# Sampled tokens out of the last product's matmuls in three of eight weight units: their rows gathered by indirect DMA and added by VectorE, which also makes the low half of those weights

## The chip, the cores and the metric

The kernel runs on one core of a Trainium2 chip. The metric is device time in microseconds (us). The kernel before took 2319.9 us, the median of 3 runs (2318.9 to 2320.13).

## The reference, cut to what matters

One layer for 256 prompt tokens and 32 sampled tokens (8 sequences of 4), 288 columns in all. It has an attention and pooling part, a norm, and then an expert layer, which takes most of the time:

```
s = einsum('chpe,hpne->chpn', q, sub_keys)     # 8 heads, 2 halves, 128 keys
ts, ti = top_k(s, 16)                          # ... then the best 16 of 256 pairs
idx  = i1 * 128 + i2                           # 8 heads x 16 experts a token, of 16384
gate = softmax(cs)
a    = einsum('cd,chkd->chk', xc, peer_u[idx])
act  = gelu(a) * gate
out  = einsum('chk,chkd->cd', act, peer_v[idx])
```

Each token uses 128 of the 16384 rows of `peer_u` and `peer_v` (2048 numbers a row, fp32). All is fp32, and the kernel keeps close to that precision.

## The kernel before, in words

**Dense instead of gathered.** The kernel does not gather. It multiplies all 16384 rows of `peer_u` with all tokens, takes gelu, writes that to a scratch tensor in HBM (`gelu_scratch`), multiplies it with a gate matrix that is zero wherever a token did not choose an expert (`gate_scratch`, made on chip from one-hot products), and multiplies the result with all of `peer_v`. The last step is the phase `peer_v`, and the change is there.

**Units.** A weight unit is 128 partitions x 2048 fp32 numbers (1 MB). `peer_v` has 128 units: 16 blocks of 1024 experts, and in each block 8 units, one for each pair of output tiles (a tile is 128 of the 2048 outputs, so there are 16 tiles and 8 pairs). A product of fp32 quality is three fp32r products: weights and activations are each split in a rounded high part and the rest. A unit is two output tiles of 24 matmuls each: 8 k-steps with `w_hi` x `b_hi` (L1412) and `w_hi` x `b_lo` (L1413), then 8 with `w_lo` x `b_hi` (L1418), each 128x128 weights on 288 columns. The result of an output tile is in one of four PSUM banks and is added to `R`.

**Who does what in `peer_v`, for unit u.** SP issues the loads of `raw` in two halves (L629), as soon as the low half of unit u-2 has been made, since `raw`, `w_hi` and `w_lo` have two buffers. ScalarE (ACT) rounds the halves to `w_hi` (L734) once PE has finished unit u-2. GpSimd (POOL) makes `w_lo = raw - w_hi` (L707). VectorE (DVE) adds a finished output tile to `R` (`take`, L1358) and makes the activations of the next block, one of eight tiles a unit (`gate`: multiply L1351, round to `b_hi` L1352, rest to `b_lo` L1353). PE waits for `hi_ready` and `lo_ready` of its unit, and for the bank it writes (`ev_dve`, the addition four output tiles back). SP also loads the next block's gelu and gate pieces (L382). All orders are written out by hand, and each engine runs its own in order.

**Before it.** The routing (top 16, chosen names and gates in `I1`, `I2`, `GA`) is done by DVE during `peer_u`; it signals `r_idx`, PE then transposes the names (L1686), DVE copies them (L1292) and begins the one-hots (L1307 to L1314) for the gate matrix (PE, L1700).

**After it.** The last 8 units run beside the start of the last norm, and after them come its sums (L597, L590, L607) and the output.

Of the kernel before, what the change touches and what calls it, by code (L numbers as in the profile page):

```python
# [118 lines left out]
def const_table():  # L119

    t = np.zeros((P, CONSTS), np.float32)

    def put(name, a):
        t[:, CONST[name][0]:CONST[name][1]] = a

    put("ident", np.eye(P))
    half = HD // 2
    inv = np.float32(10000.0) ** (-np.arange(half, dtype=np.float32) / np.float32(half))
    pos = np.concatenate([np.arange(SEQ), PAST + np.tile(np.arange(DS), DB)]).astype(np.float32)
    ang = (pos[None, :] * inv.astype(np.float32)[:, None]).astype(np.float32)  # L130
# [12 lines left out]
    put("ratio", (w / np.minimum(w, np.arange(16)[None, :] + 1)).astype(np.float32).reshape(1, -1))  # L143
    put("iota", np.arange(128)[None, :])
    return t
# [22 lines left out]
def layer(nc, xT, w_in, w_pool, w_attn, w_out, w_query, keysT, peer_u, peer_v, vecs, consts,  # L168
# [3 lines left out]
    with ctx:  # L172
# [14 lines left out]

        ah, al = (sb(name, [P, KT, T + 4], F32R)[:, :, 0:T] for name in ("a_hi", "a_lo"))
# [20 lines left out]
        F = sb("F", [P, (212863 - 4 * (6 * KT * P + KT * T + 2 * KT * (T + 4) + 2 * KT * TW + VECS + CONSTS + P)) // 4 - 32])  # L209
# [76 lines left out]
        GS, o_ab = carve(o_ab, TOKS, P)  # L286

# [25 lines left out]
        hi_ready, lo_ready = sem("hi_ready"), sem("lo_ready")  # L313
        outs_done = sem("outs_done")
# [54 lines left out]
        def block_piece(sp, b, s, n, i=None):  # L369
# [12 lines left out]
            sp.dma_start(dst, src).then_inc(blk_in[s], 16)  # L382

# [238 lines left out]
        def _(sp):  # L622
# [62 lines left out]
            with sp.Fori(0, BLOCKS // 2 - 1) as i:  # L685
                for s in range(2):
                    for j in range(8):
                        load(peer_v[16 * i + 8 * s + j], UNIT0["peer_v"] + 8 * s, 8 * i, j)
                        if j < 4:
                            block_piece(sp, 2 * i + s + 2, s, j, i)  # L690
            stream(peer_v, UNIT0["peer_v"] + 112, 16, first=112)
# [10 lines left out]
        def _(pool):  # L702
# [266 lines left out]
        def _(ve):  # L969
# [7 lines left out]
            for s in (h_prob, h_ol, g_ev):  # L977
                ve.sem_inc(s, 1)
# [310 lines left out]

            for n, dst in enumerate((I1T, I2T, gT[:, :])):  # L1290
                ve.wait_ge(r_pe, NHALF + n + 1)
                link(ve.tensor_copy(dst, ps[:, 4 + n, 0:T]))  # L1292
# [63 lines left out]
            def take(o, j, i):  # L1356
                ve.wait_ge(outs_done, OUT0["peer_v"] + i + o + 2)
                ve.tensor_tensor(R[:, j, :], R[:, j, :], ps[:, ROT[(o + 2) % 4], 0:T], ALU.add).then_inc(ev_dve, 1)  # L1358
# [7 lines left out]
            def v_block(i, s):  # L1366
# [11 lines left out]
            with ve.Fori(0, BLOCKS // 2 - 1) as i:  # L1378
                own.start(i, 32)
                for s in range(2):  # L1380
                    v_block(i, s)
                own.stop(BLOCKS // 2 - 1)
            v_block(BLOCKS // 2 - 1, 0)
# [13 lines left out]
        def _(pe):  # L1397
            def product(bank, slot, tiles, mh, ml, u, m_wait=None, cols=T):


                out = ps[:, bank, 0:cols]
                for first in range(0, len(tiles), 8):
# [11 lines left out]
                    for n, (t, k) in half:  # L1414
                        if t % 8 == 0:

                            pe.wait_ge(lo_ready, 2 * u + t // 8 + 1)
                        last = pe.matmul(out, wl[:, slot, t * P:t * P + P], mh(k), start=False,  # L1418
                                         stop=(n == len(tiles) - 1))
                last.then_inc(outs_done, 1)  # L1420
# [289 lines left out]

            def v_unit(i, s, j):
                if j == 1:

                    pe.wait_ge(ev_act, ACT_EV0["peer_u"] + 128)
                pairs("peer_v", 16 * i + 8 * s, j,
                      lambda k: bh[:, 8 * s + k, 0:T], lambda k: bl[:, 8 * s + k, 0:T], first=2)
# [7 lines left out]
            with pe.Fori(0, 4) as n:  # L1724
                for j in range(2):
                    pairs("peer_v", 112 + 2 * n, j, a_op(bh), a_op(bl), first=2)
            pe.wait_ge(act_ready, 8 * BLOCKS)
            for j in range(8):
                v_unit(BLOCKS // 2 - 1, 1, j)
# [76 lines left out]
```

## Time and profile before

| | |
|---|---|
| median of 3 runs | 2319.9 us |
| span of the profiled execution | 2318.2 us |
| PE busy | 2301.9 us (99%) |
| DVE, ACT, POOL busy | 1419.4, 882.9, 1702.8 us |
| DMA | 198 GB/s over the span |
| last product (`peer_v`) | from about 1490.4 us to about 2300 us |

The profiled execution is known by its span alone; the median of the runs shown is 1.7 us above it. The span is from the first to the last instruction of the core. "Busy" of PE is pipelined: each matmul record is longer than the distance to the next, so the distance between starts is what counts, and a group of n back-to-back matmuls that is b us long with records of m us has the distance (b - m) / (n - 1).

### The profile page before, as it was taken

To read this page: it belongs to the slowest core of one execution; us is meant where nothing else is said; L and a number is where in the kernel's file an instruction comes from. 1 tells how busy PE (TensorE), PEld (TensorE's weight loads), DVE (VectorE), ACT (ScalarE), POOL (GpSimd) and SP (SyncE) were. 2 spreads that over 40 slices of the span, in tenths; PEclk is the share of its full clock that TensorE was granted. 3 is DMA by queue.
4 is the path that set the end of the run, shared out by engine and by line. 5 is a ranking of instruction groups with operands and counts; after the bars stand their busy time and mean duration, and the time that the engine had idled before them with its cause. 6 is when DMAs were issued, how large, how long until landed. Compare 5 with 4: busy or idle time off the path is not lost.

```text
span 2318.2 us, 48204 instructions
## 1 busy us (share of the span) xinstructions
PE 2301.9 (99%) x17575; PEld 2293.4 (99%) x17575; DVE 1419.4 (61%) x2373; ACT 882.9 (38%) x1109; POOL 1702.8 (73%) x702
## 2 busy tenths in 40 slices
PE   9999999999999999999999999999999999999997
PEld 9999999999999999999999999999999999999997
DVE  3974564355569954656565640766666777666655
ACT  5444453345544443333333333333333333333334
POOL 4876677776677777677676767777777778777775
PEclk9999999999999999999999999999999999999998
DMA  7564446654455555666666668766666666666643
GB/s 255 168 200 146 145 143 206 213 173 154 146 164 194 185 191 184 217 215 211 211 209 213 208 216 257 282 205 206 209 215 220 217 213 206 208 206 217 199 164 114
DMA packets 141275, 458.25 MB, mean 198 GB/s; under 512 B 14448, under 2 KB 37232, under 8 KB 140656
## 3 DMA queue, kind: packets, MB, share of 16 engines
q1 hardware_dynamic: 116944, 416.42, 55.6%
q10 hardware_dynamic: 24264, 40.93, 4.8%
q8 instruction: 44, 0.72, 0.1%
q14 instruction: 23, 0.19, 0.0%
HBM read 416.40 MB, written 43.28 MB: 198 GB/s over the span
## 4 chain that ended last, share of the span: by engine, by line
PE 95%; DVE 4%; ACT 0%; issue 0%; ACTq 0%; DVEq 0%
PE ps L1412 30%; PE ps L1413 30%; PE ps L1418 30%; PE ps L1700 1%; DVE F L1010 1%; PE ps L1453 1%; DVE F L1011 1%; PE ps L1626 1%; PE ps L1645 0%; DVE b_lo L1024 0%; PE ps L1460 0%; DVE R L1039 0%; DVE R L1073 0%; PE ps L615 0%; ACT R L964 0%; PE ps L1551 0%
## 5 line engine op out<-in xcount | busy, mean ns | idle before, releaser
L707 POOL TENSOR_TENSOR w_lo<-raw,w_hi 128x1024 fp32r<-128x1024 f32 x692 | 1694.3, 2470 | 599.4 <-ACT w_hi L734 568.4
L734 ACT ACTIVATE w_hi<-raw 128x1024 fp32r<-128x1024 f32 x690 | 692.8, 1052 | 686.1 <-PE ps L1418 652.5
L1412 PE MATMUL ps<-a_hi,w_hi 128*128 128x288 f32 x3072 | 824.8, 295 | 0.0
L1413 PE MATMUL ps<-a_lo,w_hi 128*128 128x288 f32 x3072 | 822.6, 294 | 0.0
L1412 PE MATMUL ps<-b_hi,w_hi 128*128 128x288 f32 (+1 forms) x2432 | 655.1, 295 | 0.4 <-ACT w_hi L734 0.4
L1413 PE MATMUL ps<-b_lo,w_hi 128*128 128x288 f32 (+1 forms) x2432 | 653.0, 295 | 0.0
L1412 PEld LDWEIGHTS ps<-a_hi,w_hi 128*128 128x128 f32 x3072 | 577.7, 188 | 2.4 <-issue 2.2
L1413 PEld LDWEIGHTS ps<-a_lo,w_hi 128*128 128x128 f32 x3072 | 577.9, 188 | 0.1
L1418 PE MATMUL ps<-a_hi,w_lo 128*128 128x288 f32 x3072 | 467.2, 294 | 0.0
L1412 PEld LDWEIGHTS ps<-b_hi,w_hi 128*128 128x128 f32 x2432 | 457.1, 188 | 0.9 <-issue 0.8
L1413 PEld LDWEIGHTS ps<-b_lo,w_hi 128*128 128x128 f32 x2432 | 457.8, 188 | 0.1
L1418 PEld LDWEIGHTS ps<-a_hi,w_lo 128*128 128x128 f32 x3072 | 424.7, 188 | 0.0
L1418 PE MATMUL ps<-b_hi,w_lo 128*128 128x288 f32 (+1 forms) x2432 | 372.0, 294 | 0.0
L1418 PEld LDWEIGHTS ps<-b_hi,w_lo 128*128 128x128 f32 x2432 | 338.1, 188 | 0.3 <-POOL w_lo L707 0.3
L1358 DVE TENSOR_TENSOR R<-R,ps 128x288 f32<-128x288 f32 x240 | 103.1, 449 | 243.1 <-PE ps L1418 243.1
L906 ACT ACTIVATE F<-ps 128x288 f32<-128x288 f32 x128 | 52.5, 410 | 504.3 <-PE ps L1418 504.2
L1353 DVE TENSOR_TENSOR b_lo<-F,b_hi 128x288 fp32r<-128x288 f32 x128 | 171.3, 1338 | 4.4
L1323 DVE COPY F<-ps 128x512 f32<-128x512 f32 x72 | 49.8, 692 | 199.0 <-PE ps L1700 199.0
L1351 DVE TENSOR_TENSOR F<-F 128x288 f32<-128x288 f32 x128 | 122.7, 959 | 75.5 <-DMA F<-gate_scratch 69.2
L1352 DVE CAST b_hi<-F 128x288 fp32r<-128x288 f32 x128 | 156.6, 1223 | 4.4
L1331 DVE TENSOR_TENSOR g_stage<-ps,F 128x512 f32 (+1 forms) x72 | 81.1, 1127 | 0.1
L801 ACT ACTIVATE F<-ps,vec 128x288 f32 (+1 forms) x32 | 16.0, 501 | 111.7 <-PE ps L1418 111.7
(238 smaller groups left out, 1256.4 us busy)
## 6 DMA issues: line engine op xcount, KB each, us to landing
raw<-in_peer_u SPq DMA_DIRECT2D x256, 512.0 KB, 4.3
raw<-in_peer_v SPq DMA_DIRECT2D x256, 512.0 KB, 4.0
raw<-in_w_in SPq DMA_DIRECT2D x96, 512.0 KB, 3.9
gelu_scratch<-F ACTq DMA_DIRECT2D x32, 576.0 KB, 5.7
gate_scratch<-g_stage ACTq DMA_DIRECT2D x36, 512.0 KB, 6.0
F<-gelu_scratch SPq DMA_DIRECT2D x32, 576.0 KB, 5.7
raw<-in_w_out SPq DMA_DIRECT2D x32, 512.0 KB, 3.7
raw<-in_w_query SPq DMA_DIRECT2D x32, 512.0 KB, 3.7
```

The lines of the kernel that those rows point to most:

```text
L707: pool.tensor_tensor(wl[:, j, s], raw[:, j, s], wh[:, j, s].bitcast(F32), ALU.subtract).then_inc(lo_ready, 1)
L734: act.activation(wh[:, k, s], raw[:, k, s], ACT.Copy).then_inc(hi_ready, 1)
L906: act.activation(ST[:, j // 4, j % 4, :], ps[:, j % 2, 0:T], ACT.Gelu).then_inc(ev_act, 1)
L1323: copied = own.inc(ve.tensor_copy(GS, both[:, :, 1, :]))
L1331: ve.tensor_tensor(to[:, :, :, TOKS * j:TOKS * j + TOKS].rearrange("p a e t -> p t (a e)"), both[:, :, 0, :], GS, ALU.add).then_inc(g_ev, 1)
L1351: link(ve.tensor_tensor(a, a, g, ALU.mult))
L1352: link(ve.tensor_copy(bh[:, 8 * s + e, 0:T], AB[:, s, e, :]))
L1353: ve.tensor_tensor(bl[:, 8 * s + e, 0:T], AB[:, s, e, :], bh[:, 8 * s + e, 0:T].bitcast(F32), ALU.subtract).then_inc(act_ready, 1)
L1358: ve.tensor_tensor(R[:, j, :], R[:, j, :], ps[:, ROT[(o + 2) % 4], 0:T], ALU.add).then_inc(ev_dve, 1)
L1412: pe.matmul(out, w, mh(k), start=(n == 0), stop=False)
L1413: pe.matmul(out, w, ml(k), start=False, stop=False)
L1418: last = pe.matmul(out, wl[:, slot, t * P:t * P + P], mh(k), start=False, stop=(n == len(tiles) - 1))
```

## The change

**Which products shrink.** In each block the last 3 of the 8 units (`dj >= DENSE`, 5) multiply 256 columns, the prompt alone, in place of 288. Their additions to `R` (`take`) have 256 columns too. Block 14 (units 112 to 119) is written as two loops of two units, and there only units 117 and 119 are short (118 is multiplied with 288 columns, and 256 are added). So 14 x 3 + 2 + 3 = 47 units are short, of 128.

**Where the sampled tokens' part comes from.** The 32 tokens x 128 experts are put in 32 slots of 128 partitions. For each slot POOL issues six indirect DMAs, one for each of the 6 output tiles (128 rows of 128 numbers of `peer_v`, 64 KB), and a seventh for the 128 gelu values. Their names are worked out by DVE after the routing. DVE multiplies gelu by gate and adds the slot's rows to `ACC` (128x768). In the last block six small matmuls with a 0/1 matrix (`spread`) sum `ACC` over the partitions of a token into the columns 256 to 288 of the bank. The issues are paced by `outs_done`: 7 for 6.2 output tiles; a slot has one of two buffers (`RING`).

**Who makes `w_lo`.** POOL makes it up to the end of `peer_u` and for the last 8 units of `peer_v`. For the 120 units between DVE does (`lower`), one unit ahead, between `gate` and `take`. SP's loads wait for the new semaphore `lo_dve`; they and the block pieces keep their turn.

The diff, cut to its core:

```diff
+SPARSE = 3
+DENSE = 8 - SPARSE
+ROWS = 2 * SPARSE
+SLOTS = PH * TOPK // 4
+RING = 2
+V_LAST = 120
...
# gpsimd
-            with pool.Fori(FIRST_UNITS // 2, UNITS // 2) as i:
+            with pool.Fori(FIRST_UNITS // 2, UNIT0["peer_v"] // 2) as i:
                 for j in range(2):
                     lower(i, j)
...
+            def paced(k, r):
+                i, m = divmod(k, 5)
+                pool.wait_ge(outs_done, OUT0["peer_v"] + 1 + 32 * i + int(6.2 * (m + r / (ROWS + 1))))
+            for k in range(SLOTS):
+                n = k % RING
+                if k >= RING:
+                    pool.wait_ge(slot_used, k - RING + 2)
+                for r in range(ROWS):
+                    paced(k, r)
+                    pool.indirect_dma_start(VROWS[:, n, r * P:r * P + P], None, v_rows,
+                                            bass.IndirectOffsetOnAxis(ap=VIDX[:, k, r:r + 1], axis=0))\
+                        .then_inc(row_in[n][r], 16)
+                paced(k, ROWS)
+                pool.indirect_dma_start(GELU[:, k:k + 1], None, gelus, ...)\
+                    .then_inc(gelu_in[n], 16)
+            with pool.Fori((UNIT0["peer_v"] + V_LAST) // 2, UNITS // 2) as i:
+                for j in range(2):
+                    lower(i, j)
...
# vector
             def take(o, j, i):
+                n = v_cols(j // 2)
...
+            def lower(u, j):
+                for h in range(2):
+                    ve.wait_ge(hi_ready, 2 * (UNIT0["peer_v"] + u) + h + 1)
+                    s = slice(h * HU, h * HU + HU)
+                    ve.tensor_tensor(wl[:, j, s], raw[:, j, s], wh[:, j, s].bitcast(F32), ALU.subtract)\
+                        .then_inc(lo_dve, 1)
+            def add_slot(i, n):
+                k, b = 10 * i + n, n % RING
+                for r in range(ROWS):
+                    ve.wait_ge(row_in[b][r], 16 * (5 * i + n // RING + 1))
+                ve.wait_ge(gelu_in[b], 16 * (5 * i + n // RING + 1))
+                link(ve.tensor_tensor(GATED[:, b:b + 1], GELU[:, bass.ds(k, 1)], EG[:, bass.ds(k, 1)], ALU.mult))
+                ve.wait_ge(slot_used, k + 1)
+                ve.scalar_tensor_tensor(out=ACC, in0=VROWS[:, b, :], scalar=GATED[:, b:b + 1], in1=ACC,
+                                        op0=ALU.mult, op1=ALU.add).then_inc(slot_used, 1)
...
                 for u in range(8):
                     if u < 7:
                         gate(1 - s, u + 1)
-                    for j in range(2):
-                        take(16 * s + 2 * u + j, 2 * u + j, 32 * i)
+                    if not isinstance(i, int) or 16 * i + 8 * s + u + 1 < V_LAST:
+                        lower(16 * i + 8 * s + u + 1, (u + 1) % 2)
+                    take(16 * s + 2 * u, 2 * u, 32 * i)
+                    if u in slots and u < 7:
+                        add_slot(group, slots[u])
+                    take(16 * s + 2 * u + 1, 2 * u + 1, 32 * i)
+                    if u in slots and u == 7:
+                        add_slot(group, slots[u])
...
+                    v_block(2 * i + n, 0, {4: 5 * n, 7: 5 * n + 1}, i)
+                    v_block(2 * i + n, 1, {2: 5 * n + 2, 5: 5 * n + 3, 7: 5 * n + 4}, i)
...
# tensor
+            def v_pair(u, s, j, dj, low, final=False):
+                n = v_cols(dj)
+                for o in range(2):
+                    bank = ROT[(2 * j + o + 2) % 4]
+                    pe.wait_ge(ev_dve, DVE_EV0["peer_v"] + 2 * u + o - 3)
+                    product(bank, j % 2, [(8 * o + k, k) for k in range(8)],
+                            lambda k: bh[:, 8 * s + k, 0:n], lambda k: bl[:, 8 * s + k, 0:n], ...)
+                    if final and n < T:
+                        r = 2 * (dj - DENSE) + o
+                        if r == 0:
+                            pe.wait_ge(slot_used, SLOTS + 1)
+                        pe.matmul(ps[:, bank, SEQ:T], ACC[:, r * P:r * P + P], C("spread"), start=True, stop=True)\
+                            .then_inc(outs_done, 1)
```

**DVE, one unit.** In the kernel before, DVE has this in each unit of `peer_v`, here in block 14, written out without a loop (F is the work area with the activations and gates, ps is PSUM):

```order
L1351 TENSOR_TENSOR F<-F 128x288
L1352 CAST b_hi<-F 128x288
L1353 TENSOR_TENSOR b_lo<-F,b_hi 128x288
L1358 TENSOR_TENSOR R<-R,ps 128x288 x2
```

In the changed kernel DVE has this in a unit with a slot (unit 100, block 12), up to the first instruction of the next unit:

```order
L1457 TENSOR_TENSOR F<-F 128x288
L1458 CAST b_hi<-F 128x288
L1459 TENSOR_TENSOR b_lo<-F,b_hi 128x288
L1472 TENSOR_TENSOR w_lo<-raw,w_hi 128x1024 x2
L1465 TENSOR_TENSOR R<-R,ps 128x288
L1482 TENSOR_TENSOR F<-F 128x1
L1484 SCALAR_TENSOR_TENSOR F<-sample_rows,F 128x768
L1465 TENSOR_TENSOR R<-R,ps 128x288
L1457 TENSOR_TENSOR F<-F 128x288
```

Two subtractions of 128x1024 have come in ahead of the first addition of a tile, and in 5 of 16 units a small multiplication and a 128x768 multiply-and-add have come in between or behind the two additions.

**POOL around `peer_v`.** The changed kernel has this after the loop that made `w_lo` of all units (it is now run up to the last unit of `peer_u`):

```order
L757 REGISTER_ALU
L759 TENSOR_TENSOR w_lo<-raw,w_hi 128x1024
L768 REGISTER_ALU
L768 COMPARE_AND_BRANCH
L791 DMA sample_rows<-in_peer_v,F 128x128 x6
L795 DMA F<-gelu_scratch,F 128x1
```

The pair of DMA rows stands there 32 times, 224 issues in all; the subtractions of 120 units are gone from POOL, and those of the last 8 follow behind.

**DVE after the routing.** The changed kernel has these rows between the last row of the routing (the gates, 96x384) and the copies of the transposed names (128x288), which followed each other before:

```order
L1369 TENSOR_TENSOR F<-F 96x384
L1375 COPY F<-F 32x32 x12
L1387 CAST F<-F 128x32
L1382 TENSOR_SCALAR F<-F 128x32
L1383 TENSOR_SCALAR F<-F 128x32
L1384 CAST F<-F 128x32
L1385 CAST F<-F 128x32
L1389 SCALAR_TENSOR_TENSOR F<-F 128x32
L1390 SCALAR_TENSOR_TENSOR F<-F 128x32
...
L1394 SCALAR_TENSOR_TENSOR F<-F 128x32
L1398 COPY F<-ps 128x288 x2
```

26 small instructions have come in ahead of the copies with which the one-hots begin.

## Rows read from the trace of the kernel before

**Rows 1.** The page: busy us, share of the span and instructions of each engine

```profile
span 2318.2 us, 48204 instructions
PE 2301.9 (99%) x17575; PEld 2293.4 (99%) x17575; DVE 1419.4 (61%) x2373; ACT 882.9 (38%) x1109; POOL 1702.8 (73%) x702
```

**Rows 2.** The page: the chain that ended last, by engine and by line

```profile
PE 95%; DVE 4%; ACT 0%; issue 0%; ACTq 0%; DVEq 0%
```

**Rows 3.** Waits from 1490 to 2285 us: who waited for what, total, times, longest

```profile
ACT w_hi L734 <- PE ps L1418: 524.7, 123, 4.3
DVE R L1358 <- PE ps L1418: 243.1, 109, 2.7
POOL w_lo L707 <- ACT w_hi L734: 168.2, 125, 3.7
...
ACT w_hi L734 <- DMA raw<-in_peer_v: 5.1, 3, 3.0
```

**Rows 4.** Matmul groups of the span, by form: count, busy us, mean ns

```profile
L1418 PE MATMUL ps<-a_hi,w_lo 128*128 128x288 f32 x3072 | 467.2, 294 | 0.0
...
L1700 PE MATMUL ps<-onehots 128*128 128x256 f32 x288 | 45.4, 279 | 0.0
...
L590 PE MATMUL ps<-ones,F 128*96 128x1 f32 x18 | 1.7, 220 | 0.0
L607 PE MATMUL ps<-F 96*128 96x288 f32 x2 | 1.3, 768 | 2.1 <-DVE F L541 2.1
```

**Rows 5.** Instructions of DVE in time, 1955 to 1985 us: start, us, what

```profile
1966.43 2.39 DVE L1352 CAST b_hi<-F 128x288 fp32r<-128x288 f32 x1
1968.85 2.54 DVE L1353 TENSOR_TENSOR b_lo<-F,b_hi 128x288 fp32r<-128x288 f32 x1
...
1977.65 0.45 DVE L1358 TENSOR_TENSOR R<-R,ps 128x288 f32<-128x288 f32 x1 [1.87 <-PE ps L1418]
1978.02 0.45 DVE L1351 TENSOR_TENSOR F<-F 128x288 f32<-128x288 f32 x1
1978.51 0.31 DVE L1352 CAST b_hi<-F 128x288 fp32r<-128x288 f32 x1
1978.85 0.46 DVE L1353 TENSOR_TENSOR b_lo<-F,b_hi 128x288 fp32r<-128x288 f32 x1
...
1983.98 0.45 DVE L1358 TENSOR_TENSOR R<-R,ps 128x288 f32<-128x288 f32 x1 [2.71 <-PE ps L1418]
```

**Rows 6.** ACT and POOL in time, one unit of the same stretch

```profile
1965.06 2.01 ACT L734 ACTIVATE w_hi<-raw 128x1024 fp32r<-128x1024 f32 x2 [4.31 <-PE ps L1418]
...
1966.20 4.88 POOL L707 TENSOR_TENSOR w_lo<-raw,w_hi 128x1024 fp32r<-128x1024 f32 x2 [1.23 <-ACT w_hi L734]
```

**Rows 7.** DVE groups of the span, by form: count, busy us, mean ns

```profile
L1056 DVE TENSOR_TENSOR F<-F 128x1024 f32<-128x1024 f32 x4 | 4.9, 1218 | 0.0
...
L1016 DVE SCALAR_TENSOR_TENSOR F<-F 128x512 f32<-128x512 f32 x4 | 2.8, 692 | 0.1
...
L1228 DVE COPY tiny<-tiny 128x1 f32<-128x1 f32 x52 | 8.0, 154 | 1.8
```

**Rows 8.** DVE in time, 800 to 915 us, around the copies of the names

```profile
886.83 0.95 DVE L1292 COPY F<-ps 128x288 f32<-128x288 f32 x2 [33.74 <-PE ps L1686]
...
890.62 2.53 DVE L1294 TENSOR_TENSOR gate_lo<-gate_T,gate_hi 128x288 fp32r<-128x288 f32 x1
```

**Rows 9.** DMA of the span: queues with packets, MB, share; SP's issues to landing

```profile
q1 hardware_dynamic: 116944, 416.42, 55.6%
q10 hardware_dynamic: 24264, 40.93, 4.8%
...
raw<-in_peer_v SPq DMA_DIRECT2D x256, 512.0 KB, 4.0
```

**Rows 10.** Busy us by window: PE, PEld, DVE, ACT, POOL, then clock, DMA share, GB/s

```profile
1490.40:2285.00 794.60, 794.60 (x6027) 794.49 (x6026) 524.61 (x643) 257.54 (x263) 626.59 (x251) 1.00 0.63 209
```

More of the change, by code:

```diff
@@ L286, in layer @@
         GS, o_ab = carve(o_ab, TOKS, P)
+        E1, o_ab = carve(o_ab, SLOTS)
+        E2, o_ab = carve(o_ab, SLOTS)
+        EG, o_ab = carve(o_ab, SLOTS)
+        EU, EQ, EW = (GS[:, n, 0:SLOTS] for n in range(3))
+        ACC, o_ab = carve(head, ROWS * P)
+        VIDX, o_ab = carve(o_ab, SLOTS, ROWS)
+        AIDX, o_ab = carve(o_ab, SLOTS)
+        GELU, o_ab = carve(o_ab, SLOTS)
+        GATED, o_ab = carve(o_ab, RING)
+        VIDX, AIDX = VIDX.bitcast(U32), AIDX.bitcast(U32)
         ps = ctx.enter_context(nc.psum_tensor("ps", [P, 8, 512], F32))
@@ L684, in _, with load_v, load_with_block @@
                 block_piece(sp, j // 4, j // 4, j % 4)
[L685 to L691, printed above, removed]
+            def load_v(u, j, low, mark):
+                for h in range(2):
+                    sp.wait_ge(low, mark + h)
+                    sp.dma_start(raw[:, j % 2, h * HU:h * HU + HU], peer_v[u, :, h * HU:h * HU + HU])\
+                        .then_inc(loaded[2 * (j % 2) + h], 16)
+            def load_with_block(i, t):
+                u, s, j, i2 = 16 * i + t, t // 8 % 2, t % 8, i + t // 16
+                load_v(u, j, lo_dve, 2 * u - 3)
+                if j < 4 and not (isinstance(i, int) and u >= 112):
+                    block_piece(sp, 2 * i2 + s + 2, s, j, i2)
+            for j in range(2):
+                load_v(j, j, lo_ready, 2 * (UNIT0["peer_v"] + j) - 3)
+                block_piece(sp, 2, 0, j, 0)
+            with sp.Fori(0, BLOCKS // 2 - 2) as i:
+                for t in range(2, 18):
+                    load_with_block(i, t)
+            for t in range(2, 18):
+                load_with_block(BLOCKS // 2 - 2, t)
+            with sp.Fori(57, V_LAST // 2 + 1) as i:
+                for j in range(2):
+                    load_v(2 * i + j, j, lo_dve, 4 * i + 2 * j - 3)
+            for u in range(V_LAST + 2, 128):
+                load_v(u, u % 2, lo_ready, 2 * (UNIT0["peer_v"] + u - V_LAST - 2) + 1)
             for e in range(0, KT, 2):
@@ L1364, in _, with v_block @@
             ve.wait_ge(y_init, 1)
-            def v_block(i, s):
+            lower(0, 0)
+            def v_block(i, s, slots, group=None):
                 ve.wait_ge(blk_in[1 - s], 64 * (i + s + 1))
@@ L1397, in _, with product @@
         def _(pe):
-            def product(bank, slot, tiles, mh, ml, u, m_wait=None, cols=T):
+            def product(bank, slot, tiles, mh, ml, u, m_wait=None, cols=T, low=None, ends=True):
                 out = ps[:, bank, 0:cols]
+                lo_sem, lo_base = low or (lo_ready, 2 * u)
                 for first in range(0, len(tiles), 8):
@@ L1723, in _ @@
             pe.wait_ge(act_ready, 8 * BLOCKS - 8)
-            with pe.Fori(0, 4) as n:
-                for j in range(2):
-                    pairs("peer_v", 112 + 2 * n, j, a_op(bh), a_op(bl), first=2)
+            for part in (0, DENSE // 2), (DENSE // 2, 4):
+                with pe.Fori(*part) as n:
+                    for j in range(2):
+                        u = 112 + 2 * n + j
+                        v_pair(u, 0, j, 2 * part[0] + j, (lo_dve, 2 * u))
             pe.wait_ge(act_ready, 8 * BLOCKS)
             for j in range(8):
-                v_unit(BLOCKS // 2 - 1, 1, j)
+                u = V_LAST + j
+                v_pair(u, 1, j, j, (lo_ready, 2 * (UNIT0["peer_v"] + u - V_LAST)), final=True)
                 if j == 1:
```

77 lines of the change are left out of this document (63 added, 14 removed).

## The prediction

> **What bounds the kernel now.** I read the page's busy line first. PE is busy 2301.9 us of a span of 2318.2 us [rows 1]. The chain that ended last is 95% PE and 4% DVE [rows 2]. So a change pays only by what it takes from PE or from the chain's ends, and it costs what it makes PE wait. Next come the waits inside the last product [rows 3]. There ACT waits for PE (524.7 us), DVE waits for PE (243.1 us), POOL waits for ACT (168.2 us), and no wait of PE is in the list. In the window 1490.4 to 2285 us PE is busy every microsecond of 794.6, at a granted clock of 1.00, which is the higher of its two levels, 2.4 GHz [rows 10]. The product is one dense stream of matmuls with all other work beneath it.
>
> The distance between matmuls is the price that matters. The group of 288 columns has 3072 matmuls in 384 groups of 8: 467.2/384 = 1.217 us a group, less one record of 0.294, over 7: 131.8 ns. The gate products of 256 columns are 288 in 72 groups of 4: (45.4/72 - 0.279)/3 = 117.2 ns [rows 4]. Both go by the column (0.458 ns), and both change their weights with each matmul. A unit is 48 matmuls: 6.33 us. The additions of one output tile in [rows 5], at 1977.65 and 1983.98 us, are that far apart.
>
> **The change, part by part.**
>
> *Shorter matmuls.* 47 units x 48 = 2256 matmuls go from 131.8 to 117.2 ns: 14.6 x 2256 = 32.9 us less on PE. A short unit is 48 x 0.1172 = 5.63 us.
> The Trainium skill prices the distance otherwise. Its page "TensorE: Matmul & The Clock Gate" (Back-to-back issue gap) has columns / 2.4 GHz + 2.5 ns for matmuls alone, 13.3 ns less for 32 columns, so 30 us. The same section has a sustained 81 ns at 128 columns and 131 ns at 512, an estimate of 4.2 ns for 32 columns and 9 us in all. The distances of [rows 4] contradict the second, 131.8 ns at 288 columns already, and lie above the first; I keep the rows.
>
> *Six small matmuls* (128x32, fp32) in the last block. The nearest are 128x1 fp32 (18 in 1.7 us, some 0.09 each) and the 96x288 fp32 pair (1.3 us, 0.65 each) [rows 4]. So 6 x 0.09 to 0.65 is 0.5 to 3.9 us. I take 0.15 each, near the first: +0.9 us.
>
> *DVE's load in the product.* With POOL quiet, a tile's three activation instructions take 1978.02 to 1979.31, so 1.29 us [rows 5]. While POOL works they are held: 2.39 and 2.54 us for what is else 0.31 and 0.46 [rows 5], as long as POOL's 2.44 (4.88 for two) [rows 6]. The added `lower` is 2 x 1.218 (128x1024, two inputs) [rows 7] = 2.44. Two additions are 0.90. So a unit costs DVE 1.29 + 2.44 + 0.90 = 4.63 us. A slot costs 0.154 for the small one, 0.955 for 128x768 (halfway between 0.692 at 512 and 1.218 at 1024 [rows 7]) and some 0.1 of order, 1.2 us; 5 in 16 units make 0.38. That is 5.0 us a unit, against (5 x 6.33 + 3 x 5.63)/8 = 6.07 us of PE. DVE fits with 1.07 us to spare, since POOL's subtractions, which held it up, are gone from this stage.
>
> *Is `w_lo` in time?* After PE starts unit u, DVE has the last addition (0.45), a tile (1.29), and the first half (1.22): 2.96 us, the second half 4.2. ACT's halves are done at about 1.1 and 2.1 [rows 6], earlier. PE wants the first half only 16 matmuls into unit u+1: 5.63 + 1.88 = 7.5 us. The slack is 4.5 us, and a slot's 1.2 is inside it. Behind a late `lower` stand the additions, which PE needs only three output tiles later (8.4 us). POOL finished the halves at 3.6 and 6.0 us (start 1966.20, 4.88 long, against 1965.06), so SP's loads start 0.6 and 1.8 us sooner than before. They have 11.3 - 4.2 = 7.1 us in two short units, where they had 12.7 - 6.0 = 6.7. Nothing is late, at no cost. If that cover went, SP's next load and the block pieces queued behind it would go late too, and ACT behind them.
>
> *POOL's gathers*, 224 of them. No row shows an indirect DMA. Pacing and ring allow 35 in 16 units, so 97.1/35 = 2.77 us each. Bounds from far rows: far below a POOL instruction, nothing; above, its 128x1024 subtraction, 2.5 us. Both fit, and I take some 1 us, hidden. The tightest slot is the fifth of each group. Its gelu is issued when 30 of 32 output tiles are done and used after the 32nd: 5.63 us, against 1 us of issue and 4.0 us to landing, which 512 KB take [rows 9]; 64 KB should take less. At 2.5 us of issue DVE would wait 0.9 us, six times at most, inside the 4.5 us of slack.
>
> *Index arithmetic after the routing*: 26 small instructions of DVE. Free-standing they are 0.154 us and a link each, 5 us. Held by POOL each time they are 2.5 us each, 65 us. DVE then waited 33.7 us for PE's transposes [rows 8], and 26 such instructions need some 20 us: in each 6.33 us POOL is quiet for 1.3 us, room for about 6, and two more slip in between its halves. Hidden; at the upper end the one-hots would be some 30 us late and PE with them. Index copies ahead of the first activations fall in DVE's wait for the gate pieces.
>
> *Ends.* The first `lower` falls in the wait at the product's start. The last 8 units and the norm are as before. 0.
>
> *Sum.* 2318.2 - 32.9 + 0.9 = 2286.2 us of span, and with the 1.7 us by which the median is above it: 2288 us.
>
> **The rivals.**
>
> *A. POOL's descriptor work holds DVE* (the other side). POOL's instructions do hold DVE today [rows 5, 6]. If each gather holds DVE for h, DVE loses 2.19 h a unit (35 in 16 units). The spare 1.07 us is used up at h = 0.49 us; from 0.63 us the 0.31 us a unit that the short matmuls give (32/104) is lost too, and it is slower. At 1 us it is 1.12 us x 104 units = +116, some 2405 us. Against it: a gather reads one column of names, where the subtraction reads 2 x 1024, so the hold should be short.
> The Trainium skill has it the other way round too. "SBUF — State Buffer" (SBUF: two separate sides) says that VectorE's two-port instructions lock GpSimd out of writing descriptors. Here only the rounding to `b_hi`, 0.31 us a unit, is near that kind, and no row of before shows descriptors written, so it changes no term.
>
> *B. The gathers are slow.* Above 2.77 us each, DVE waits for rows at the head of its queue, `lower` and the additions behind it, and PE behind those. The gain is gone at 2.77 + 32/224 = 2.91 us; at 3.5 us it is 224 x 0.73 = +163, 2450 us. For it: POOL makes them in software, 128 rows at a time. Against: its longest row is 2.5 us with 2048 numbers read.
> "DMA: Bandwidth & Descriptors" of the Trainium skill (Anatomy of one DMA) gives about 2.0 us for such a DMA, mostly completion and not issue; by that price B doesn't happen.
>
> *C. The gathers crowd the weight loads.* 224 x 128 = 28672 small packets. Queue q10's packets take 4.8% x 16 x 2318/24264 = 73 ns each [rows 9]; at that price it is 131 us of each DMA engine in 630 us, 0.21 over the share of 0.66 that 0.63 [rows 10] becomes at the faster pace. By bytes (192 x 64 KB = 12.6 MB at the 49.5 us per MB of q1) it is 0.06. At 0.87, loads come late now and then; ACT already waited 5.1 us in three places [rows 3]. A wait of 1 us beyond the slack in a third of the 47 short units is 5 to 20 us: 2293 to 2308.
>
> *D. The change doesn't shorten what it should.* If the weights' load set the distance, PE would gain nothing: 2320 us; by the flatter rule above 2311. [Rows 4] speak against both.
>
> **How the numbers follow.** Forecast 0.62 (its own range 2284 to 2298); A 0.13, of which 0.03 still gains; B 0.08; C 0.12, all but 0.01 a gain; D 0.05, half of it the small gain. Under 0.2% (4.6 us) this kernel's measurement tells nothing from no change. Faster: 0.62 + 0.03 + 0.11 + 0.02 = 0.78. Same: 0.05. Slower: 0.17, from A and B. The range goes from 2284 (all 33 us, small matmuls free, and a us or two of spread) to 2320: above that are the worse parts of A and B, some 0.15.
>
> **What would show it.** Right: matmuls of 256 columns 117 ns apart; PE without waits in the product, 6.33 and 5.63 us units; DVE's `w_lo` subtractions near 1.22 us and its activations near 0.31 and 0.46; the copies of the names still waiting some 10 us for PE. Wrong: DVE's instructions over 1 us while POOL issues; waits of DVE on `sample_rows` landing; ACT waiting for `raw`; PE waiting for `w_lo` or the additions; POOL over 2.8 us a gather.

## The result, and the profile after

The changed kernel took 2305.2 us (median; 2303.09 to 2306.78), the kernel before beside it 2319.7. The ratio is 0.9937 with a 95% interval of 0.9923 to 0.9951. It is faster, but by 14.5 us where 31.7 were forecast: the sign is right and the time lies inside the range, and more than half of the gain did not come. The profiled execution has a span of 2302.1 us, 16.1 below the one before, where the sum had 32.0.

The page of the changed kernel, in the parts that answer to [rows 1, 2] and to the queues of [rows 9]:

```profile
span 2302.1 us, 48482 instructions
PE 2280.8 (99%) x17587; PEld 2271.8 (99%) x17587; DVE 1486.8 (65%) x2711; ACT 884.1 (38%) x1109; POOL 1363.1 (59%) x686
...
PE 93%; DVE 5%; issue 1%; DMA 1%; ACT 1%; SPq 0%; DVEq 0%; ACTq 0%
...
q1 hardware_dynamic: 116944, 416.43, 55.6%
q10 hardware_dynamic: 24264, 40.93, 4.8%
q0 software_dynamic: 7168, 12.61, 1.8%
```

PE still sets the time. The gathers are q0: 7168 packets with 12.61 MB, 1.8% of the engines' span, where the prediction's rival C had 28672 packets.

Waits of the changed kernel inside the last product, 1480 to 2290 us (total, times, longest), against [rows 3]:

```profile
ACT w_hi L816 <- PE ps L1562: 455.4, 111, 8.3
POOL sample_rows L791 <- PE ps L1562: 290.2, 149, 5.3
DVE R L1465 <- PE ps L1562: 134.1, 88, 2.4
...
PE ps L1562 <- DVE w_lo L1472: 4.2, 2, 2.1
ACT w_hi L816 <- DMA raw<-in_peer_v: 2.8, 2, 1.7
```

The row of PE is new: it now waits twice for `w_lo`. Groups of the same kernel by form (count, busy us, mean ns, idle before), 1490 to 2270 us:

```profile
L1472 DVE TENSOR_TENSOR w_lo<-raw,w_hi 128x1024 fp32r<-128x1024 f32 x239 | 281.6, 1219 | 10.6 <-ACT w_hi L816 10.5
...
L791 POOL DMA_INDIRECT sample_rows<-in_peer_v,F x192 | 219.3, 1142 | 328.3 <-PE ps L1562 290.2 <-issue 38.1
...
L1459 DVE TENSOR_TENSOR b_lo<-F,b_hi 128x288 fp32r<-128x288 f32 x120 | 55.1, 459 | 4.2
...
L1458 DVE CAST b_hi<-F 128x288 fp32r<-128x288 f32 x120 | 44.6, 371 | 4.1
L1484 DVE SCALAR_TENSOR_TENSOR F<-sample_rows,F 128x768 f32<-128x768 f32 x32 | 32.6, 1019 | 3.8
```

The durations that the prediction used for DVE and POOL are here nearly as forecast: the subtraction 1219 ns (1218), `b_lo` 459 (460), the slot 1019 (955), a gather 1142 (some 1 us). The rounding to `b_hi` averages 371 against 310: 36 of the 120 have no gather beside them and take 310 to 313 ns, the 84 that overlap one average 398, at most 546. POOL waited most of the time for its pacing. The windows view has PE busy 785.78 of 790 us here, with a clock of 1.00 and a DMA share of 0.68; the missing 4.2 are the two waits:

```profile
1490.00:2280.00 790.00, 785.78 (x6145) 785.20 (x6144) 570.50 (x961) 263.10 (x271) 298.00 (x240) 1.00 0.68 227
```

**The first wait.** DVE in time in the changed kernel, 1686 to 1701 us:

```profile
1689.90 0.16 DVE L1482 TENSOR_TENSOR F<-F 128x1 f32 x1 [0.37 <-DMA F<-gelu_scratch,F]
1690.19 1.02 DVE L1484 SCALAR_TENSOR_TENSOR F<-sample_rows,F 128x768 f32<-128x768 f32 x1
1696.00 0.46 DVE L1457 TENSOR_TENSOR F<-F 128x288 f32<-128x288 f32 x1 [4.79 <-PE ps L1562]
1696.50 0.33 DVE L1458 CAST b_hi<-F 128x288 fp32r<-128x288 f32 x1
...
1698.44 2.35 DVE L1472 TENSOR_TENSOR w_lo<-raw,w_hi 128x1024 fp32r<-128x1024 f32 x2
```

Between the slot and the first activation DVE does nothing for 4.8 us. The view puts this down to PE, but the activation needs nothing that PE has just done. What stands between the two in the program is the end of DVE's loop over the blocks: its compare-and-branch is recorded at 1690.28 and the next record of DVE is at 1695.77, 5.5 us from start to start, of which the first 0.9 lie under the slot. The same hole follows at 1890 us; at the third pass the loop is left and the branch takes 0.11 us. The start of a block in the middle of a pass has no hole (slot at 1792.01, activation at 1792.94).

The DMA view of the first hole, 1690.3 to 1695.8 us, has one packet (8 KB) of a queue that carries instructions:

```profile
q14 instruction: 1, 0.01, 0.4%
```

It starts at 1693.80 us, 3.5 us after the branch. The second hole (branch at 1889.78) has one at 1893.42. From 1585 to 2200 us, where the kernel before branches back six times, its trace has no packet of this queue. PE in time at the same place:

```profile
1697.31 0.30 PE L1557 MATMUL ps<-b_lo,w_hi 128*128 128x288 f32 x1
1699.71 1.40 PE L1562 MATMUL ps<-b_hi,w_lo 128*128 128x288 f32 x8 [2.11 <-DVE w_lo L1472]
1700.91 0.44 PE L1556 MATMUL ps<-b_hi,w_hi 128*128 128x288 f32 x1
1701.15 0.44 PE L1557 MATMUL ps<-b_lo,w_hi 128*128 128x288 f32 x1
```

PE stands for 2.1 us and makes the eight `w_lo` matmuls in 1.2 us. Then it runs 240 ns a matmul instead of 132, until 1704.27 us. The granted clock of that stretch is 0.50, the lower level (1.2 GHz):

```profile
1700.90:1704.30 3.40, 3.40 (x17) 3.40 (x16) 3.33 (x7) 0.00 (x0) 0.95 (x1) 0.50 0.83 273
```

After the second wait (it begins at 1896.91) one distance is 235 ns, and the clock stays up.

**The distances.** The rest is not in any wait. The starts of the matmuls in the traces, averaged over a stretch, are apart as follows (ns; taking other pairs into the mean moves a figure by up to 0.3, in all kernels alike):

| kernel | gate matrix and product before, 900 to 1380 us | last product, 288 columns | 256 columns |
|---|---|---|---|
| before | 131.8 | 131.9 | (117.2 in groups of four, [rows 4]) |
| changed | 132.6 | 132.5 | 119.0 |

The 900 to 1380 us stretch has no instruction of the product that was changed, and is 0.6% slower all the same.

The same is seen, and more exactly, in the length of two stages. These are the times between the starts of the first and the last matmul, in us: for the stage of the gate matrix, its one-hot products; for the last product, its 6144 matmuls on `b_hi` and `b_lo`. The kernels in the lower rows are those of the experiments below.

| kernel | stage of the gate matrix | last product |
|---|---|---|
| before | 482.7 | 810.4 |
| changed | 486.0 | 791.0 |
| again | 486.0 | 790.7 |
| align | 482.7 | 786.5 |
| unroll | 486.0 | 784.8 |
| align and unroll | 482.7 | 780.2 |
| short only | 482.7 | 779.2 |
| before, shifted (160 B) | 486.0 | 814.4 |
| before, shifted by 64 B | 483.6 | 813.5 |
| F shifted | 486.0 | 810.4 |

### The profile page after: what moved, and what is told of

It is laid out like the page before. It is cut to its first block, busy times and chain, and to the rows that moved or that the text cites. A ratio compares the mean times of both kernels' runs of the same rounds, so it can differ in the third digit from the quotient of the medians.

```text
span 2302.1 us, 48482 instructions
## 1 busy us (share of the span) xinstructions
PE 2280.8 (99%) x17587; PEld 2271.8 (99%) x17587; DVE 1486.8 (65%) x2711; ACT 884.1 (38%) x1109; POOL 1363.1 (59%) x686
## 3 DMA queue, kind: packets, MB, share of 16 engines
q0 software_dynamic: 7168, 12.61, 1.8%
## 4 chain that ended last, share of the span: by engine, by line
PE 93%; DVE 5%; issue 1%; DMA 1%; ACT 1%; SPq 0%; DVEq 0%; ACTq 0%
PE ps L1562 29%; PE ps L1556 29%; PE ps L1557 29%; PE ps L1845 1%; DVE F L1092 1%; DVE F L1093 1%; PE ps L1598 1%; PE ps L1771 1%; DMA F<-gelu_scratch,F 1%; PE ps L1790 0%; DVE b_lo L1106 0%; PE ps L1605 0%; DVE R L1121 0%; PE ps L646 0%; ACT R L1046 0%
## 5 line engine op out<-in xcount | busy, mean ns | idle before, releaser
L759 POOL TENSOR_TENSOR w_lo<-raw,w_hi 128x1024 fp32r<-128x1024 f32 x452 | 1094.7, 2445 | 546.9 <-ACT w_hi L816 515.7
L1556 PE MATMUL ps<-b_hi,w_hi 128*128 128x288 f32 (+2 forms) x2432 | 637.2, 292 | 0.4 <-ACT w_hi L816 0.4
L1557 PE MATMUL ps<-b_lo,w_hi 128*128 128x288 f32 (+2 forms) x2432 | 634.8, 291 | 0.0
L791 POOL DMA_INDIRECT sample_rows<-in_peer_v,F x192 | 219.3, 1142 | 328.3 <-PE ps L1562 290.2
L1562 PE MATMUL ps<-b_hi,w_lo 128*128 128x288 f32 (+2 forms) x2432 | 364.6, 291 | 4.2 <-DVE w_lo L1472 4.2
L1562 PEld LDWEIGHTS ps<-b_hi,w_lo 128*128 128x128 f32 x2432 | 331.9, 188 | 4.9 <-DVE w_lo L1472 4.7
L1472 DVE TENSOR_TENSOR w_lo<-raw,w_hi 128x1024 fp32r<-128x1024 f32 x240 | 282.7, 1219 | 11.5 <-ACT w_hi L816 11.5
L1465 DVE TENSOR_TENSOR R<-R,ps 128x288 f32<-128x288 f32 (+1 forms) x240 | 104.0, 438 | 159.0 <-PE ps L1562 134.1
L1457 DVE TENSOR_TENSOR F<-F 128x288 f32<-128x288 f32 x128 | 62.3, 486 | 77.0 <-DMA F<-gate_scratch 64.8
L1459 DVE TENSOR_TENSOR b_lo<-F,b_hi 128x288 fp32r<-128x288 f32 x128 | 67.2, 525 | 4.4
```

The lines of the kernel that those rows point to most:

```text
L759: pool.tensor_tensor(wl[:, j, s], raw[:, j, s], wh[:, j, s].bitcast(F32), ALU.subtract).then_inc(lo_ready, 1)
L791: pool.indirect_dma_start(VROWS[:, n, r * P:r * P + P], None, v_rows, bass.IndirectOffsetOnAxis(ap=VIDX[:, k, r:r + 1], axis=0))\
L1457: link(ve.tensor_tensor(a, a, g, ALU.mult))
L1459: ve.tensor_tensor(bl[:, 8 * s + e, 0:T], AB[:, s, e, :], bh[:, 8 * s + e, 0:T].bitcast(F32), ALU.subtract).then_inc(act_ready, 1)
L1465: ve.tensor_tensor(R[:, j, 0:n], R[:, j, 0:n], ps[:, ROT[(o + 2) % 4], 0:n], ALU.add).then_inc(ev_dve, 1)
L1472: ve.tensor_tensor(wl[:, j, s], raw[:, j, s], wh[:, j, s].bitcast(F32), ALU.subtract)\
```

## The experiments

Each kernel below ran with the kernel before beside it (2319.7 to 2319.9 us); the ratios are to that.

**Again.** The changed kernel, unaltered.

> The changed kernel once more, unaltered. Both theories of the slower matmuls (S: the place of the tensors behind the longer constants, 32 bytes off a multiple of 64; L: VectorE's heavier load and the other loop code) say that the distances repeat: 288 columns 132.6 ns in the stage of the gate products and 132.5 in the last product, 256 columns 119.0 ns, and two waits of PE for w_lo of about 2.3 us where VectorE's loop turns back. Median 2303 to 2307 us. If the distances come out at 131.8 and 117.2, the difference was of that one execution and both fall.

Measured: 2302.25 us, ratio 0.9925 (0.9911 to 0.9938), span 2301.0. The distances came out the same (132.6, 132.5, 119.0), and PE waited 2.2 and 1.7 us for `w_lo` at the same two places. All of it belongs to the kernel and not to one execution.

**Align.** The changed kernel has 33 more constant columns (`token`, `spread`: 132 B) ahead of the work tensors, and F ends 8 columns shorter. The tensors behind the constants moved by 160 B: `b_hi` and `b_lo`, which PE streams in the last product, the one-hots and F. `a_hi` and `a_lo` stand ahead of them and moved in no kernel here. Here 31 unused columns make the move 256 B.

```diff
-                  ("ratio", PG * 16), ("iota", 128), ("token", 1), ("spread", NS)):
+                  ("ratio", PG * 16), ("iota", 128), ("token", 1), ("spread", NS), ("pad", 31)):
```

> The changed kernel with 31 more columns in the table of constants, so that the tensors behind it (b_hi, b_lo, the work area, the one-hots) begin at multiples of 64 bytes, as they did before. S: matmul distances go back to 131.8 ns (288) and 117.2 ns (256), which gives 2.8 us in the stage of the gate products and 4 + 3.7 us in the last product, so 8 to 10 us less than the unaltered change, some 2295 us; the two waits at VectorE's loop end stay. L: the same 132.5 and 119.0 ns and no change of the time.

Measured: 2297.55 us, ratio 0.9908 (0.9893 to 0.9923), span 2294.1, so 7 to 8 us less than the changed kernel's two profiles. The distances are 131.8 again from 900 to 1380 us and 131.8 in the product, and the short matmuls fell to 118.0. Both waits for `w_lo` stay (2.2 us each). Nothing but the place of tensors changed.

**Unroll.** DVE's loop over the blocks of the last product written out, so that there is no branch back.

```diff
-            with ve.Fori(0, 3) as i:
-                own.start(i, 64 + 10)
+            for i in range(3):
...
-                own.stop(3)
```

> The changed kernel with VectorE's loop over three times four blocks written out, so no branch back. Theory F (the branch back of the long loop body takes 5.4 us, which makes w_lo late): both waits of PE (2.3 us each) and the 14 matmuls at half clock behind the first (1.5 us) are gone, 6 us less, some 2299 us, and VectorE has no pause over 2 us between a slot and the next activations at about 1691 and 1891 us. Rival (VectorE is late there through the slot and the two tiles of activations that meet at a block's start, not through the branch): the waits stay.

Measured: 2297.15 us, ratio 0.9903 (0.9888 to 0.9918), span 2295.5, 5.5 to 6.6 less than the changed kernel's. DVE and PE in time at the place of the hole:

```profile
1689.78 1.02 DVE L1484 SCALAR_TENSOR_TENSOR F<-sample_rows,F 128x768 f32<-128x768 f32 x1
1690.72 0.45 DVE L1457 TENSOR_TENSOR F<-F 128x288 f32<-128x288 f32 x1
1691.20 0.31 DVE L1458 CAST b_hi<-F 128x288 fp32r<-128x288 f32 x1
...
1691.92 0.45 DVE L1457 TENSOR_TENSOR F<-F 128x288 f32<-128x288 f32 x1
...
1693.13 2.35 DVE L1472 TENSOR_TENSOR w_lo<-raw,w_hi 128x1024 fp32r<-128x1024 f32 x2
...
1697.15 1.23 PE L1560 MATMUL ps<-b_hi,w_lo 128*128 128x288 f32 x8
```

The hole is gone, and PE has no wait in the product. The distances stay long (132.6, 132.5, 119.0). So the two losses are apart: one is the branch, the other the place of tensors. The rows also show how much time there was to spare at this place: the first half of `w_lo` is done at 1694.35 us and PE wants it at 1697.15, 2.8 us later. A block's start has two tiles of activations ahead of its first subtraction, where the other units have one.

**Before, shifted.** The kernel before with 33 unused constant columns, and F cut by 8, as in the changed kernel.

```diff
-                  ("ratio", PG * 16), ("iota", 128)):
+                  ("ratio", PG * 16), ("iota", 128), ("pad", 33)):
```

> The kernel before with 33 unused columns in the table of constants, which puts the tensors behind it where the changed kernel has them, 32 bytes off a multiple of 64. S: 288 columns at 132.6 ns in the stage of the gate products (+2.8 us) and 132.3 to 133 ns in the last product (6144 matmuls, +4 to +6 us): 2326 to 2329 us, slower than before by 0.3 to 0.4%. L: no difference, 2319.7 us within 1 us.

Measured: 2326.78 us, ratio 1.0030 (1.0018 to 1.0043), 7 us slower, with no instruction changed. The `w_lo` matmuls of the last product (1500 to 2230 us), first in the kernel before, then in this one:

```profile
L1418 PE MATMUL ps<-b_hi,w_lo 128*128 128x288 f32 x1844 | 280.1, 294 | 0.0
```

```profile
L1418 PE MATMUL ps<-b_hi,w_lo 128*128 128x288 f32 x1840 | 281.5, 295 | 0.0
```

Four fewer matmuls take 1.4 us more. By the starts the distance is 132.6 and 132.5 instead of 131.8 and 131.9, and the two stages are 3.3 and 3.9 us longer.

**Short only.** The kernel before with the 47 short units and nothing else. It leaves out the sampled tokens' part of those units (no gathers, no slots, no small matmuls), POOL makes all of `w_lo`, and no tensor moves.

> The kernel before with one edit: the same 47 units multiply 256 columns and add 256. The sampled tokens' part of these tiles is left out, so this is the price of the short matmuls alone, with GpSimd making w_lo and no gathers. If the distance at 256 columns is the 117.2 ns that the gate products showed, 2256 x 14.6 = 32.9 us: 2286.8 us. If it is the 118.0 ns that the aligned changed kernel showed in the product, 2256 x 13.8 = 31.1 us: 2288.6 us. Rival (118 ns comes from VectorE's load and the gathers): 117.2 ns here.

Measured: 2288.4 us, ratio 0.9863 (0.9847 to 0.9878), span 2286.3, 31.9 below the kernel before. The distances are 131.8 and 118.0. This is what the shortening is worth by itself: 13.8 ns x 2256 = 31.1 us; the last product is 31.2 us shorter.

**Align and unroll.** Both repairs of the changed kernel at once.

> The changed kernel with both repairs: tensors at multiples of 64 bytes and VectorE's loop written out. If the two losses are independent: 288 columns at 131.8, 256 at 118.0 ns, no wait of PE in the product, 5 to 7 us + 5 to 6 us less than the change unaltered, some 2291 us. If they overlap (the late w_lo came from slower matmuls or the other way round), 2295 us or more.

Measured: 2289.41 us, ratio 0.9867 (0.9852 to 0.9882), span 2287.3. The short `w_lo` matmuls of the last product, 1500 to 2230 us, for both repairs and for *unroll* alone (busy us, mean ns):

```profile
L1560 PE MATMUL ps<-b_hi,w_lo 128*128 128x256 f32 x704 | 97.3, 280 | 0.0
```

```profile
L1560 PE MATMUL ps<-b_hi,w_lo 128*128 128x256 f32 x704 | 98.4, 282 | 0.0
```

For eight matmuls that is 1.106 us and 1.118. No wait of PE is left in the product. It stands 1.0 us above *short only*, which has none of the added work: 224 gathers, 32 slots and 240 subtractions moved to DVE cost nothing, and the six small matmuls take what is left. From the forecast 2288 it is 1.4 us away.

**Before, shifted by 64 B.** The same edit as the shift above, with 16 unused columns.

> The kernel before with 16 unused columns in the table of constants: the tensors behind it move by 64 bytes, still at multiples of 64, but at a multiple of 128 where they were 64 off one. If what counts is the place within 64 bytes: distances of 131.8 ns and 2319.7 us as before. If any move of these tensors against the others changes the distances, slower as with 160 bytes, 2322 us or more.

Measured: 2323.3 us, ratio 1.0014 (1.0005 to 1.0023), 3.5 us slower, where the idea of the place within 64 B had expected nothing. The distances are 132.1 (900 to 1380 us) and 132.3. The idea that only a place off a multiple of 64 B costs was wrong. In the kernel before `b_hi` stands 64 B past a multiple of 128, after 256 B more still there, and after 64 B or 160 B not; that is as much as three places can say.

**F shifted.** The kernel before with `b_hi` and `b_lo` where they were, and F, which holds the one-hots, moved by 160 B and 42 columns shorter.

```diff
+        sb("unused", [P, 40])
...
```

> The kernel before with 160 unused bytes a partition between b_lo and the work area: the work area and the one-hots move by 160 bytes, b_hi, b_lo and all tensors ahead stay. If the place of what PE streams decides: the stage of the gate products (one-hots moved) is slow as with everything moved, 132.6 ns, +2.9 us, and the last product (b_hi, b_lo in place) is at 131.8: 2322.6 us. If the place of VectorE's work area decides, both stages are slow and it is 2326 to 2327 us, as with everything moved.

Measured: 2322.94 us, ratio 1.0014 (1.0005 to 1.0023), some 3 us slower. The distance is 132.6 from 900 to 1380 us, where PE streams one-hots out of F for part of the time, and 131.8 in the last product, whose streams had not moved. So in the last product it is the place of `b_hi` and `b_lo` that counts: it is 3.9 us longer where they moved by 160 B and as long as before where F alone moved. In the stage of the gate matrix moving F is enough for the whole 3.3 us. But that is not shown to be the place of what PE streams: of the 52 matmuls of a unit there, only four stream one-hots, and they lose some 10 ns together; the other 48 stream `a_hi` and `a_lo`, which did not move, and lose 37. Why a place costs 0.3 to 1 ns a matmul stays open in both stages.

**Before, with a long loop.** The kernel before with DVE's loop of two blocks a pass made two passes of six. The trace has 444 rows of DVE from one branch to the next in place of 151; the changed kernel has 512.

```diff
-            with ve.Fori(0, BLOCKS // 2 - 1) as i:
-                own.start(i, 32)
-                for s in range(2):
-                    v_block(i, s)
+            with ve.Fori(0, 2) as i:
+                own.start(i, 96)
+                for n in range(3):
+                    for s in range(2):
+                        v_block(3 * i + n, s)
```

> The kernel before with VectorE's loop in the last product run twice over three bodies instead of seven times over one (its text is three times as long, 441 instruction rows for 147), nothing else. Theory F (a branch back over a long body is what takes 5.4 us): the one branch back takes about 5 us where it took 0.3, and since VectorE has slack in this kernel the time stays 2319.7 us. Rival (the pause belongs to what else the changed kernel does at that place): it stays 0.3 us.

Measured: 2319.78 us, ratio 1.0 (0.999 to 1.001). DVE in time at the loop's end, first in the kernel before (its six branches back have 0.29 to 0.33 us to the next record), then in this one:

```profile
1592.23 0.46 DVE L1351 TENSOR_TENSOR F<-F 128x288 f32<-128x288 f32 x1 [0.17 <-issue]
```

```profile
1794.03 0.46 DVE L1358 TENSOR_TENSOR R<-R,ps 128x288 f32<-128x288 f32 x1 [2.71 <-PE ps L1421]
1799.33 1.01 DVE L1351 TENSOR_TENSOR F<-F 128x288 f32<-128x288 f32 x1 [4.85 <-issue]
```

The branch back takes 4.99 us with the long body, and here too one 8 KB packet of q14 (instruction) lies in the hole, at 1797.29 us, 3.2 us after the branch. It costs the time nothing here, since POOL makes `w_lo` and DVE's activations are wanted only a block later. In the changed kernel the same 5 us are on the way to `w_lo`.

**More pairs.** With both repairs, 4, 5 and 6 of the 8 pairs shortened. Block 14 is written out in all, so that its units are short too: 64, 80 and 96 units. A slot has 8, 10 and 12 rows.

```diff
-SPARSE = 3
+SPARSE = 5
...
-            for part in (0, DENSE // 2), (DENSE // 2, 4):
...
+            for dj in range(8):
+                v_pair(112 + dj, 0, dj % 2, dj, (lo_dve, 2 * (112 + dj)))
```

> Both repairs, four of eight pairs short (8 gathers of rows and one of gelu for each slot), and block 14 written out so that all its short units are short: 64 short units, 17 more. If PE's column count still sets the time: 17 x 48 x 13.8 = 11.3 us less, 0.4 us for two more small matmuls, 2280 us. If the gathers (45 in 16 units, 2.1 us each allowed, 1.2 us each in the changed kernel) or VectorE (5.1 of 6.0 us a unit) become late, PE waits and the time stays at 2290 us or rises.

> As the kernel with four short pairs, but five: 80 short units, 10 gathers of rows and one of gelu a slot. By columns: 16 x 48 x 13.8 = 10.6 us less, 0.4 more for two small matmuls: 2271 us. Limits: the gathers are 55 in 16 units of 5.9 us, 1.7 us each allowed, 1.2 us each measured so far plus some 0.3 between them; VectorE 5.3 of 5.9 us a unit. If one of them is late, PE waits for w_lo or for the banks and the time is 2275 us or more.

> Six short pairs: 96 short units, 13 gathers a slot. By columns 2261 us. The gathers have 65 in 16 units, 1.44 us each, which is what they need with the time between them (1.2 + 0.3): I expect GpSimd to fall behind here, VectorE to wait for rows, and 2265 us or more; if there is room after all, 2261 us.

Measured: 2281.41 us with four (ratio 0.9833, 0.982 to 0.9846), 2275.72 with five (0.9807, 0.9794 to 0.9821) and 2331.52 with six (1.0053, 1.0039 to 1.0066). A short unit is worth 48 x 13.8 ns = 0.66 us. Four pairs have 17 short units more than *align and unroll*, 11.2 us less 0.4 for two small matmuls, and gave 8.0; five have 16 more again, 10.2 us net, and gave 5.7. By the stages the fourth pair paid nearly in full inside the last product, 10.3 us, and lost 2.4 behind it: from the product's last matmul to the end of the span are 19.9 us against 17.4, and the cause of that is open. The fifth took 3.5 us from the product, and 5 us of what is missing are in one place, where PE stops between the matmuls of a unit and the clock falls:

```profile
1530.00:1538.00 8.00, 5.81 (x24) 4.84 (x24) 3.63 (x6) 1.88 (x3) 5.37 (x6) 0.65 0.76 240
```

Eight us hold 24 matmuls there, where 68 are the rule at 118 ns. Waits of the five-pair kernel, 1480 to 2290 us:

```profile
POOL sample_rows L791 <- PE ps L1560: 96.6, 72, 16.6
POOL sample_rows L791 <- issue: 76.6, 242, 1.3
...
ACT w_hi L816 <- DMA raw<-in_peer_v: 12.7, 9, 2.4
...
DVE F L1482 <- DMA F<-gelu_scratch,F: 11.0, 7, 2.1
```

and of the six-pair kernel, 1480 to 2330 us:

```profile
POOL sample_rows L791 <- issue: 115.2, 326, 15.5
...
ACT w_hi L816 <- remote: 99.3, 15, 13.8
...
POOL sample_rows L791 <- PE ps L1560: 37.9, 42, 3.0
...
DVE F L1482 <- DMA F<-gelu_scratch,F: 22.0, 7, 4.6
...
PE ps L1554 <- issue: 13.7, 21, 1.0
...
PEld ps L1560 <- DVE w_lo L1472: 12.1, 8, 3.6
PE ps L1560 <- DVE w_lo L1472: 9.5, 6, 3.4
```

POOL's waits for its pacing shrink from 290 us (three pairs) to 97 and 38: with six it is behind, DVE waits for slots, and `w_lo` comes late. 384 gathers at 1.2 us and some 0.3 from one to the next are 576 of the 770 us on average, so POOL would keep up if the average decided; that it is late because each slot's work comes in bursts is a guess. The windows view of the six-pair kernel has PE without work for 37 of 820 us, and a clock of 0.97:

```profile
1490.00:2310.00 820.00, 782.61 (x6153) 770.29 (x6152) 592.97 (x962) 263.75 (x271) 535.75 (x432) 0.97 0.70 233
```

Of these 37 us PE waits 9.5 for `w_lo`. The larger part, 26.6 us in 49 pieces of at most 1.0 us, stands under "issue": PE stops between matmuls of one unit, as in the five-pair kernel at 1530 us, and waits for nothing that the profile shows. So the late `w_lo` explains only a part of the loss with six pairs; what else PE lacks is open.

The best kernel of the study is the one with five pairs: 2275.7 us, 1.9% below the kernel before and 1.3% below the changed one.

## Why the prediction was right and wrong

**Right: what bounds.** PE sets the time, and it goes by the columns. *Short only* gained 31.9 us of span where 32.9 were forecast for it. Rival D (no shortening) is out.

**Right: DVE fits, and POOL doesn't hold it.** The step had 1.29 us for the activations, 2.44 for `lower`, 0.90 for the additions. The rows have 0.452 + 0.371 + 0.459 = 1.28, 2 x 1.219 and 0.90. While POOL subtracted, the activations of the kernel before averaged 938, 1215 and 1344 ns; a gather holds the rounding to `b_hi` by 0.09 us on average and 0.24 at most, and the rest not at all, also in the five-pair kernel. Rival A, which needed 0.49 us a gather, is out.

**Right: the gathers are hidden.** 1.14 us each, with 2.77 to be had. Rival B is not in this kernel, but it is a part of what the six-pair kernel runs into. Rival C was priced with 28672 packets; there were 7168, the DMA share was 0.68, and ACT waited 2.8 us for `raw` in the whole product. Its waits begin to show at five pairs (12.7 us, and 11.0 of DVE for gelu).

**Right: the index arithmetic.** DVE's wait for the transposed names was 33.7 us [rows 8]. This is it in the changed kernel, 850 to 900 us:

```profile
DVE F L1398 <- PE ps L1831: 12.1, 1, 12.1
```

So the 26 instructions took 21.6 us; some 20 had been forecast, and "some 10 us" of wait to be left.

**Wrong: "Is `w_lo` in time? ... Nothing is late, at no cost."** In an ordinary unit the slack of 4.5 us was right: in *unroll*, the first half of `w_lo` is done 4.3 to 5.5 us before PE wants it, slots included. Two things were left out. The first unit of a block has a second tile of activations (1.2 us) ahead of its subtraction, and in all blocks but two only 2.1 to 3.1 us are left there. And DVE's loop has a branch at the end of four blocks, right at such a place: it keeps DVE idle for 4.8 us, where 2.8 were to spare. The difference, 2.0, is the wait that the rows have, twice (2.1 us). Together with the matmuls at the lower clock after the first wait that cost 6.2 us of the last product (791.0 against 784.8). By the matmuls' starts the two waits are 4.5 us of it and the lower clock 1.5. The trace of before could have shown the branch only as a hint: its own, with a short body, takes 0.3 us.

**Wrong: the distances in the sum.** The sum kept 131.8 ns for all matmuls that were not shortened and took 117.2 for the shortened. Two things were off. First the place, a term that the sum did not have at all: the diff adds 33 constant columns ahead of `b_hi`, `b_lo` and F. That costs 3.3 us in the stage of the gate matrix and 4.5 in the last product, 7.8 in all; *align* took back 7 to 8. Then the size: 117.2 came from gate products in groups of four, and in the product itself 256 columns take 118.0 at the old place (*short only*); (14.6 - 13.8) x 2256 = 1.8 us. Inside the product the six small matmuls took 1.1 us where 0.9 were forecast.

**The account** of the 15.9 us of span that did not come (32.0 - 16.1): two waits and the clock 6.2, place 7.8, size 1.8, small matmuls 0.2, together 16.0. Each of the first two was taken away by itself and both together, and the result met the forecast within 1.4 us. That the time of the changed kernel fell inside the range is luck: the range reached up to 2320 us to cover the rivals (C's 2293 to 2308 us among them), and none of those came true.

**The rule weighed against the rows.** The Trainium skill's "TensorE: Matmul & The Clock Gate" (Back-to-back issue gap) has, by its formula for a matmul alone, 13.3 ns less for 32 columns. The measured difference is 131.8 - 118.0 = 13.8 ns, nearer to it than the 14.6 of [rows 4]. Its absolute figures are some 9 ns lower than the traces' distances.

## What to carry to other kernels

When work moves to an engine that was not on the path, look for the ends of that engine's loops: a branch back that cost nothing before is now inside a slack, and its price can be 0.3 us with a short body and 5 with a long one. Work out the slack at the tightest place of the loop, here a block's first unit, and not for the ordinary unit. A change that adds a constant or a buffer moves all tensors behind it; run the old kernel with that padding alone before the rest of a diff is blamed or praised for a few tenths of a per cent. Take a price from the same instruction pattern in the same stage, and not from short groups elsewhere.

## What the runs showed of the hardware that was not expected

- DVE's branch back took 0.29 to 0.33 us with 151 rows in the body, 4.99 with 444, and 4.8 to 5.6 with 512 (from the branch to the next record). Each of the long ones has one 8 KB packet of the instruction queue q14 in it, 2.8 to 3.6 us after the branch, and the short ones have none; packets of that queue in the middle of the long body (1791.02 us) go with no hole. This fits a loop body that has to be fetched again on the way back, but no run tested it.
- Moving `b_hi` and `b_lo` by 64 or 160 B made a matmul of 288 columns 0.5 to 0.6 ns longer in distance in the last product, and 160 B made one of 256 columns 1.0 ns longer; a move by 256 B changed nothing. Moving F by 160 B made the stage of the gate matrix 3.3 us longer, mostly on matmuls whose own streams had not moved. In all this was 3.5 to 8 us of the kernel. It was tried with three moves only.
- A wait of PE of 2.1 us was followed once by 3.4 us at the lower clock, and once by none.
- A gather of POOL held DVE's rounding 128x288 (398 ns beside one, 310 without), and none of its instructions with two inputs.
- An indirect DMA of 128 rows of 512 B took POOL 1.14 to 1.22 us on average in all kernels that had it. From three pairs to five, 128 gathers more made 4096 packets more, 2048 of them under 512 B: 16 small ones and 16 of 4 KB a gather, so eight rows to a packet.
